# A two-layer mixer block on one core: norm sums on other engines, rows of their own for one branch, and a last-row-last order

## The reference

```python
def _rmsnorm(x, g):
    x32 = x.astype(jnp.float32)
    y = x32 * lax.rsqrt(jnp.mean(jnp.square(x32), axis=-1, keepdims=True) + EPS)
    return (y * g.astype(jnp.float32)).astype(x.dtype)

def _layernorm(x, g, b):
    mu = jnp.mean(x32, axis=-1, keepdims=True)
    var = jnp.mean(jnp.square(x32 - mu), axis=-1, keepdims=True)
    y = (x32 - mu) * lax.rsqrt(var + EPS) * g.astype(jnp.float32) + b.astype(jnp.float32)
...
    ys = (_short_conv(a_b, a_c, a_u, conv_a) @ w_a_out,
          y_b @ w_b_out,
          (jax.nn.gelu(r_g) * rec) @ w_c_out,
          _conformer_conv(d_v, d_g, conv_d, conv_d_b, ln_d_g, ln_d_b) @ w_d_out)
    out = _merge(gl, ys, w_out)
...
        x = x + gt1 * o
        x = x + gt2 * _swiglu(_modulate(x, g_ffn[l], sh2, sc2), w_ffn_in[l], w_ffn_out[l])
...
    return _rmsnorm(x, g_final)
```

## Time and profile before

| What | Value |
| --- | --- |
| median of 3 runs | 2089.33 us (2087.57 to 2090.14) |
| profiled execution | 2084.34 us |
| span in it | 2082.5 us |
| TensorE busy | 2036.4 us, 98% |
| VectorE, ScalarE, GpSimd busy | 1105.7, 877.5, 817.1 us |
| granted TensorE clock | 0.996 of full speed |

### The profile page before, as it was taken

The page is one execution under the profiler, slowest core; times in us unless marked ns, Lnnn a source line. Parts: engine busy times, 40 slices in busy tenths (PEclk is TensorE's granted clock), DMA queues, the critical chain, the costliest instruction groups (busy, mean ns, idle before and its releaser), DMA issues.

```text
span 2082.5 us, 30660 instructions
## 1 busy us (share of the span) xinstructions
PE 2036.4 (98%) x11738; PEld 1700.8 (82%) x11738; DVE 1105.7 (53%) x2031; ACT 877.5 (42%) x1369; POOL 817.1 (39%) x355
## 2 busy tenths in 40 slices
PE   5999999999999999999999999999999999999998
PEld 3778788888877778777777778777999999999998
DVE  5896454567788632123111111479755887644555
ACT  4786344232222333134221222369755434545444
POOL 1003322343434334334343343510446887344443
PEclk9999999999999999999999999999999999999999
DMA  7222211222222222664634422322333455454554
GB/s 312 93 81 82 79 52 55 90 90 101 83 99 81 101 63 100 242 243 182 242 122 170 173 82 101 132 91 82 121 123 121 171 194 184 161 171 160 190 188 142
DMA packets 38705, 278.45 MB, mean 134 GB/s; under 512 B 4416, under 2 KB 4416, under 8 KB 5312
## 3 DMA queue, kind: packets, MB, share of 16 engines
q1 hardware_dynamic: 38592, 276.87, 37.2%
HBM read 275.80 MB, written 1.05 MB: 133 GB/s over the span
## 4 chain that ended last, share of the span: by engine, by line
PE 89%; DVE 5%; ACT 2%; DMA 1%; issue 1%; POOL 1%; SPq 0%; DVEq 0%; ACTq 0%; POOLq 0%
PE PS L473 86%; PE PS L562 2%; DVE PS L1270 1%; ACT WH L838 1%; PE PS L737 1%; POOL WL L433 1%; DVE ZL L1267 1%; DMA RAW<-in_stream 1%; DVE TMP L1273 0%; DMA X<-in_xT 0%; DMA CD<-in_lruw 0%; DVE PS L1267 0%; DVE CD L1270 0%; ACT TMP L838 0%; ACT ZH L838 0%
## 5 line engine op out<-in xcount | busy, mean ns | idle before, releaser
L433 POOL TENSOR_TENSOR WL<-RAW,WH 128x1024 fp32r<-128x1024 f32 x336 | 805.8, 2418 | 1240.8 <-ACT WH L838 1240.8
L473 PE MATMUL PS<-HH,WH 128*128 128x512 f32 (+1 forms) x2272 | 799.5, 352 | 8.2 <-DVE HL L1270 3.4
L473 PE MATMUL PS<-HL,WH 128*128 128x512 f32 (+1 forms) x2272 | 778.2, 343 | 0.0
L473 PE MATMUL PS<-HH,WL 128*128 128x512 f32 (+1 forms) x2272 | 778.0, 342 | 0.0
L838 ACT ACTIVATE WH<-RAW 128x1024 fp32r<-128x1024 f32 x416 | 417.4, 1052 | 723.8 <-PE PS L473 687.8
L473 PEld LDWEIGHTS PS<-HH,WH 128*128 128x128 f32 x2272 | 428.1, 188 | 79.0 <-issue 23.3
L473 PEld LDWEIGHTS PS<-HL,WH 128*128 128x128 f32 x2272 | 428.5, 189 | 57.4 <-issue 5.5
L473 PEld LDWEIGHTS PS<-HH,WL 128*128 128x128 f32 x2272 | 428.0, 188 | 55.6
L473 PE MATMUL PS<-ZH,WH 128*128 128x512 f32 (+1 forms) x992 | 337.7, 340 | 6.3 <-DVE ZL L1267 4.7
L473 PE MATMUL PS<-ZH,WL 128*128 128x512 f32 (+1 forms) x992 | 335.5, 338 | 0.0
L473 PE MATMUL PS<-ZL,WH 128*128 128x512 f32 (+1 forms) x992 | 335.5, 338 | 0.0
(11 more groups left out here) (165 smaller groups left out, 1504.4 us busy)
## 6 DMA issues: line engine op xcount, KB each, us to landing
RAW<-in_stream SPq DMA_DIRECT2D x208, 1024.0 KB, 4.8
CD<-in_modw SPq DMA_DIRECT2D x42, 1024.0 KB, 7.7
CD<-in_lruw SPq DMA_DIRECT2D x2, 2048.0 KB, 8.1
X<-in_xT SPq DMA_DIRECT2D x2, 1024.0 KB, 7.3
S<-in_modw SPq DMA_DIRECT2D x2, 1024.0 KB, 13.0
G<-in_modw SPq DMA_DIRECT2D x2, 1024.0 KB, 21.0
RAW<-in_modw SPq DMA_DIRECT2D x1, 1024.0 KB, 16.0
TMP<-in_modw SPq DMA_DIRECT2D x1, 1024.0 KB, 17.9
```

The lines of the kernel that those rows point to most:

```text
L433: nc.gpsimd.tensor_tensor(WL[:, a:b], RAW[:, a:b], WH[:, a:b].bitcast(F32), ALU.subtract)\
L473: return nc.tensor.matmul(out, lhs, rhs, start=start, stop=stop)
```

## The change

It has seven parts.

1. **Opening norm.** ScalarE squares into five buffers instead of two; TensorE adds the eight rows itself with eight all-ones float32 matmuls of 512 columns, after six more small ones issued early (`keep_warm(6)`); root and reciprocal are of 128x512 and there are no diagonals and no spread. The table for the root is loaded ahead of the squares.
2. **Other norms.** The diagonals are made by ScalarE (`diagonals` in `norm_root`, so ahead of the `high` that follows), no longer by VectorE.
3. **Order.** In the first slabs of w_out and ff_out (both tiles from Z) rows 0 to 6 of both tiles come first, then row 7 of both.
4. **Branch b in layer 2.** It has rows of its own in Z (offset NX), copied row by row during c_out.
5. **a_cu in layer 1.** The output banks are given free by the first product, not by the last low part.
6. **LayerNorm.** VectorE adds the 8 rows (and the 8 squares) with 7 additions each; TensorE keeps one all-ones matmul for each.
7. **a_out in layer 2.** GpSimd forms both halves of WL.

```diff
-POOL_WHOLE = ("c_in", "kv", "q", "d_in", "c_out", "b_out", "a_cu", "a_b", "w_out")
+POOL_WHOLE = ("c_in", "kv", "q", "d_in", "c_out", "b_out", "a_cu", "a_b", "a_out", "w_out")
...
-            pe.wait_ge(L[0]["n1_s"].sem, KC - 1)
-            token_sums(tmp(1), NT, True, True).then_inc(L[0]["n1_p"].sem, 1)
-            spread(L[0]["n1_v"].sem, NT).then_inc(L[0]["n1_p"].sem, 1)
+            keep_warm(6)
+            for k in range(KC):
+                pe.wait_ge(L[0]["n1_a"].sem, k + 1)
+                mm(bank(7), ONES, SQUARES[k % len(SQUARES)], k == 0, k == KC - 1)\
+                    .then_inc(L[0]["n1_p" if k == KC - 1 else "n1_s"].sem, 1)
...
+                if before is not None and ops[0][0] in (Z, Z2):
+                    for rows in (range(nk - 1), range(nk - 1, nk)):
+                        for t, (z, w) in enumerate(ops):
+                            for k in rows:
+                                if t == 0:
+                                    before(k)
...
+                                last = products(s, t, z, w, k, nk)
...
-                for k in range(KC):
-                    last = mm(bank(4, W), ONES, row(CD, k, W), k == 0, k == KC - 1)
-                last.then_inc(lp.sem, 1)
+                pe.wait_ge(lv.sem, lv.at(0, f"a{KC - 1}"))
+                mm(bank(4, W), ONES, tmp(4, 0, W), True, True).then_inc(lp.sem, 1)
                 stage(l, "a_out", [(H, W), (Z, W)], pairs=(1, 2))
-                pe.wait_ge(la.sem, la.at(0, f"q{KC - 1}"))
-                for k in range(KC):
-                    last = mm(seqs(bank(5, W), seqs_of(l)), ONES, padded(k, seqs_of(l)), k == 0, k == KC - 1)
-                last.then_inc(lp.sem, 1)
+                pe.wait_ge(lv.sem, lv.at(0, f"v{KC - 1}"))
+                mm(bank(5, W), ONES, tmp(4, 0, W), True, True).then_inc(lp.sem, 1)
...
+            def diagonals(inverse, m):
+                act.wait_ge(inverse, 1)
+                for c in range(m):
+                    fn(tmp(1, c * P, (c + 1) * P), IDENT, ACT.Identity, scale=tmp(0, m + c, m + c + 1)).then_inc(inverse, 1)
...
+                        gate("co")(n, s, m)
+                        fn(row(ZH, n, W, NX), row(CD, n, W), ACT.Copy).then_inc(a["bz_h"].sem, 1)
...
+                    if l:
+                        dve.wait_ge(a["bz_h"].sem, a["bz_h"].at(n, "z"))
+                        z_low(n, W, row(CD, n, W), NX).then_inc(a["bz_l"].sem, 1)
...
                     tt(seq[:, 0:C, PAD:PAD + NX], seqs(tmp(s, 0, W), C), seqs(bank(2 * s + 1, W), C), MUL)\
-                        .then_inc(*((slab_out[s], 1) if l else (sv.sem, 1)))
+                        .then_inc(slab_out[s], 1)
...
-                        z_low(n, W, tmp(2 + s, 0, W)).then_inc(slab_out[s], 1)
+                        z_low(n, W, tmp(2 + s, 0, W)).then_inc(sv.sem, 1)
...
+                def row_sums(name, at, part):
+                    for k in range(1, KC):
...
+                        tt(seqs(tmp(4, 0, W) if k == KC - 1 else part, C), at(0) if k == 1 else seqs(part, C), at(k), ADD)\
+                            .then_inc(lv.sem, 1)
+                dve.wait_ge(a["cd"].sem, KC * TAPS_D)
+                row_sums("a", lambda k: seqs(row(CD, k, W), C), bank(4, W))
                 stage(l, "a_out", gated("ao"), some=(0, 1))
...
                     tt(row(CD, k, W), row(CD, k, W), bank(4, W), SUB).then_inc(lv.sem, 1)
+                row_sums("v", lambda k: padded(k, C), bank(6, W))
                 stage(l, "a_out", gated("ao"), some=(1, 2))
```

More of the change, by code:

```diff
@@ L514, in slab @@
                     return
+                if before is not None and ops[0][0] in (Z, Z2):
[4 more added lines that the diff above has]
+                                    before(k)
+                                if t == 0 and k == KC // 2 and halves == 1:
+                                    second_half(m, s)
+                                last = products(s, t, z, w, k, nk)
+                            if nk - 1 in rows:
+                                last.then_inc(tile_done[s], 1)
+                            elif t == 0:
+                                for slot, u in mods:
+                                    mod_products(slot, u)
+                    mod_columns_of(mods)
+                    return
                 for j, t in enumerate(order):
@@ L517, in slab @@
                     for k in range(nk):
-                        if before is not None and z is Z and (t == 0 or ops[0][0] is not Z):
+                        if before is not None and z in (Z, Z2):
                             before(k)
@@ L795, in _ @@
                 for s in range(2):
-                    slab(b, s, [(H, W), (Z, W)], order=(1, 0) if s else (0, 1), halves=1)
-                stage(l, "b_out", [(H, W), (Z, W)], before=lambda k: pe.wait_ge(a["bz_l"].sem, a["bz_l"].at(k, "z")))
+                    slab(b, s, [(H, W), (Z, W)], order=(1, 0) if s and l == 0 else (0, 1), halves=1)
+                stage(l, "b_out", [(H, W), (Z2 if l else Z, W)], before=lambda k: pe.wait_ge(a["bz_l"].sem, a["bz_l"].at(k, "z")))
                 stage(l, "a_cu", [(H, W), (H, W)])
@@ L1298, in low, with z_low @@
                 tt(WL[:, x], RAW[:, x], WH[:, x].bitcast(F32), SUB).then_inc(lo_done[1][s], 1)
-            def z_low(n, w, src):
-                return tt(row(ZL, n, w), src, row(ZH, n, w).bitcast(F32), SUB)
-            def inverse(done, chunks):
-                V.reciprocal(tmp(0, chunks, 2 * chunks), tmp(0, 0, chunks)).then_inc(done, 1)
-                dve.wait_ge(done, 1)
-                for c in range(chunks):
-                    ts(tmp(1, c * P, (c + 1) * P), IDENT, tmp(0, chunks + c, chunks + c + 1), None, MUL).then_inc(done, 1)
+            def z_low(n, w, src, at=0):
+                return tt(row(ZL, n, w, at), src, row(ZH, n, w, at).bitcast(F32), SUB)
             def decay_rates(l):
@@ L1379, in _ @@
                         dve.wait_ge(x_loaded[s], 16)
-                    sums, squared = a["n1_s"].sem, a["n1_a"].sem
-                    for k in range(1, KC):
-                        dve.wait_ge(squared, k + 1)
-                        if k > 1:
-                            dve.wait_ge(sums, k - 1)
-                        tt(tmp(1), tmp(1), SQUARES[k % 2], ADD).then_inc(sums, 1)
                     rows = G[:, :].rearrange("p (k n) -> p k n", n=GW)
@@ L1704, in _ @@
                     conv_d(conv_taps("c_out", n))
[L1705 removed]
+                    if n == KC - 1 and l == 0:
                         for k in range(KC):
```

96 lines of the change are left out of this document (55 added, 41 removed).

## The result

The changed kernel takes 2065.54 us (median of 4 runs, 2062.7 to 2067.43) beside 2088.45 us for the kernel before (4 runs, 2087.09 to 2090.14): a ratio of 0.9889, 95% interval 0.9872 to 0.9906, or 22.9 us less by the medians. Forecast were 27.3 us less, 2062 us.

The account below looks back on a forecast made before the run. TensorE, busy 98%, was taken as the bound, so only less work or fewer waits help. Terms -11.3 - 3.3 - 6.5 - 2.6 - 3.5 - 2.2 + 2.15 = -27.3 us from 2089.3 gave 2062 us, range 2056 to 2071.

Parts of the forecast that it names:

- LayerNorm, layer 1: 14 of 16 all-ones records go, twice, with VectorE's additions covered and nothing new late: -11.3 us.
- My price of a record: One all-ones record in layer 1's LayerNorm costs TensorE 6.47/16 = 0.404 us.
- a_cu, branch b, order: Waits for low parts go: layer 1's a_cu -3.5 us, layer 2's b_out -2.6; Z's row 7 asked for later, -2.2.
- Opening: Round 0 starts near 18 us, round 1 at 23.3, bound by DMA: -6.5 us, taken from -5.2 to -7.2.
- Diagonals: Norms between stages: `high` now waits for ScalarE's diagonals; +1.1 us, +0.75 and +0.3, sum +2.15 us.
- LayerNorm, layer 2, and GpSimd's double share: Layer 2's row sums win -3.3 us of 5.7, TensorE standing some 3.4 us at tile 6; double share costs 0.
- Price 0: GpSimd forming both weight halves in layer 2's a_out costs nothing, with 0.9 us of cover.
- My bound of -1.5 us: Layer 2's LayerNorm wins only this if branch d's low parts overlap GpSimd's longer work; they took 7.83 us.
- signs that I had named as wrong: TensorE waiting for TMP at the all-ones matmul, for WL in layer 2's a_out, or a granted clock below 0.99.
- The clock: Rival, slower than before: the standstill at layer 2's tile 6 keeps the clock low; one dip costs 1.7 us; chance 0.02.
- The lock: Rival: each low part in c_out waits for a whole GpSimd half, 2.4 us; total 2072 us; chance 0.03.
- Layer 2 gives back its gains: Rival: faster TensorE runs into the weights' loop, losing 3.3 + 2.6 + 2.0 us; total 2070 us; chance 0.10.

Follow-up runs that it names:

- norm1_by_tensor: The changed kernel with layer 1's norm alone back to TensorE's own sums, mean and variance; 2078.38 us, ratio 0.9948.
- diag_dve: The changed kernel with the diagonals of the norms before ff_in and of layer 2's first norm made by VectorE again; 2062.26 us, ratio 0.9869.
- norm2_by_tensor: The changed kernel with both sums of layer 2's norm back to TensorE, GpSimd's share as changed; 2066.24 us, ratio 0.9888.
- after_again: The changed kernel run and profiled once more on another chip, nothing edited; 2063.96 us, ratio 0.9882.
- after: The first profiled execution of the changed kernel, the slowest of its four; 2067.43 us.
- half_dve: The changed kernel with a_out's low weight parts of layer 2 half on GpSimd and half on VectorE, as before; 2061.47 us, ratio 0.9869.
- warm7: The changed kernel plus seven all-ones products of 256 columns in the standstill of layer 2's LayerNorm; 2065.44 us, ratio 0.9889.

## Why the prediction was right, and where it was wrong

The time is inside the range and the sign and size are right, 22.9 to 25.5 us by the medians of two chips against 27.3. Step by step:

- *LayerNorm, layer 1.* Right, and slightly small: 12.0 us in two steps of 6.0 for 11.3, confirmed by norm1_by_tensor (the table's 12.2 has 0.1 us that norm1_by_tensor shows too). My price of a record was too low. The records start 0.43 us apart (720.50 to 720.93 in the kernel before), but the product behind the last one starts 0.03 us after it and is itself the longer, 0.80 instead of 0.40 us, and it did so in the earlier trace rows too. So 6.47/16 leaves part of the last record out; 14 x 0.43 is 6.0. In layer 2 it is 0.215 us and 3.0 for my 2.85. No wait for TMP stands there; the cover for VectorE's sums was as counted.
- *a_cu, branch b, order.* Right within 0.1, 0.1 and 0.3 us.
- *Opening.* The mechanism is right: round 0 at 19.31 (forecast near 18), round 1 at 24.18 (23.3), round 3 at 36.37 (35.3 to 37.3), with the DMA as the bound. It is -5.8 us where the lower clock fell into rounds 0 or 1, which wait for transfers anyway, and -3.9 where it reached into c_in's first slab. Of the 11 traces of kernels with the warm-up, 6 gained 5.3 to 6.0 us here and 5 gained 3.4 to 4.0. Both ends are within my bounds (0 to -7.5), but -3.9 is outside the -5.2 to -7.2 that I took, which had no price for a lower clock behind the rounds; -6.5 was at the favourable side.
- *Diagonals.* +0.9 us in layer 1 (forecast +1.1), and this is partly luck. By diag_dve the diagonals themselves cost 1.6 us there; the norm without them is 0.65 us shorter than in the kernel before, where the lower clock (951.07 to 954.49 us) made TensorE's spread 1.92 us long, for 1.16 in diag_dve, and VectorE's rows stood behind it. I had not counted that gain. Before ff_in of layer 2 it is +1.5 to +1.9 for +0.75: the lower clock lay there as well in both traces and made the first slab 0.6 us longer, which I had not counted.
- *LayerNorm, layer 2, and GpSimd's double share.* Here the prediction was wrong: -3.3 and 0 forecast, +2.6 and -0.5 measured. The step on the row sums holds by itself: the two steps of 2.9 to 3.0 us came, and TensorE stands 3.31 us at slab 6 (forecast 3.4), so -3.2 us at slab 6; norm2_by_tensor against after_again shows 3.4 us for the sums. The reciprocal's 0.45 us came too: slab 6 stands 0.4 to 0.7 us better with GpSimd's whole share than with half (after and after_again against half_dve). The step that failed is "Price 0" for the double share. I counted cover for the weights only, and they were never late there (no wait for WL in a_out). What I left out is who else is on SBUF. Of the eight low parts of Z for d_out, one met a GpSimd instruction in the kernel before (its half from 1807.75) and all took 4.97 us; four met one when GpSimd worked for all but 1.6 us of them, and they took 9.49 us. TensorE waited 1.87 us, and the clock fell behind it for another 1.5 us. My bound of -1.5 us named this overlap, but sized it by the 7.83 us of the earlier trace rows and had no price for the clock. The pairs of the second table put the double share at 3.7 us, and at 3.2 to 3.9 where both sums are there and the fall behind S is taken off. None of the signs that I had named as wrong came (no wait for TMP or for WL there, a granted clock of 0.994 over the run), so they would not have caught this.
- *The clock.* The prediction put a fall behind the standstill at 1.7 us and within the range. It came in 4 of 6 traces with the full standstill, at 1.4 to 2.4 us each; behind the wait for ZL it came in 7 of 7, at 0.9 to 1.5 us. It never stayed low. That is part of the shortfall, and no rival held it as a cost of more than one place.
- *The lock.* Its mechanism is what happened; its place and price were wrong, and I gave it 0.03. The reading against it was a mean: 0.98 us for a low part in the earlier trace rows is five of 0.41 us, one of 1.13 and two of 2.62 and 2.57, and the long ones end 0.28 us behind the end of a GpSimd instruction of 2.5 to 2.7 us. So it is for every low part of 256 columns out of CD in all 13 traces, and the other way too: a GpSimd instruction that starts just ahead of such an end takes 2.5 to 2.6 us instead of 2.4. The Trainium skill, "SBUF — State Buffer", section "Who interferes with whom", has a VectorE instruction with two SBUF inputs and a GpSimd one that reads SBUF exclude each other for the whole of an instruction; the traces agree. But a low part waits only for what is left of the one instruction that it meets. In c_out each came 0.8 us before GpSimd's first half ended, took 1.10 us and was in time, so part 4 lost nothing of what this rival priced. In d_out's rows, where I priced nothing, three whole GpSimd instructions stood in the way.
- *Layer 2 gives back its gains.* Only in a trifle: one new wait for WL in a_cu, 0.25 us and a restart, and +0.6 us in all over b_out to a_b.

What stays open: why the clock falls behind one standstill of 3.3 us and not behind the next of the same length; why it fell behind the 1.85 us wait for ZL each time, while the kernel before kept its clock behind the 1.87 us wait at b_out and the 1.66 us wait in w_out; and whether warm7's seven products helped, since after_again kept its clock without them. Nor is it known what starts or ends the slow pace of the ff stages.

## What to carry to other kernels

Moving work to an idle engine is free only if the instructions that will now run beside it are looked at too: list the VectorE instructions with two SBUF inputs that fall into GpSimd's new stretch, and count the GpSimd instructions that they will meet, not the VectorE ones. Each one met costs the rest of its length, here up to 2.2 us, and a mean over a merged row hides this; look at the single lengths. Then follow it up to the wait that ends last. A wait of TensorE of 2 to 3 us is to be priced with the lower clock that may follow it, here 1 to 2.4 us more when it came. And a saving on TensorE is worth nothing where another chain ends last anyway: the variance's sums in layer 2 took 2.9 us off TensorE, slab 6 started no earlier, and they opened a standstill behind which the clock fell in 4 of 6 traces.

## What the runs showed that I had not expected

The granted clock falls to the lower level for 3.4 us, sometimes for 6.8, after stretches in which TensorE had stood or was thinly used: behind the 1.85 us wait for ZL in every one of 7 traces, behind 3.3 to 3.7 us of standstill in 4 of 6, and not once in those 33 us in the 4 traces where neither wait was there. The length of a wait alone does not decide it: behind 1.87 us at b_out the kernel before kept its clock. In the opening it matters where it lands: in a round that waits for a transfer it costs nothing, in the first slab behind it 2 us.

At a granted clock of 1.00, products of 256 columns can start 0.120 us apart instead of 0.117 for hundreds in a row; it came in the ff stages of some executions and not of others of the same kernel, and is worth up to 3.2 us of 2065. A single trace of each kernel would have put it down to the change.

A row of a merged timeline can hide two kinds of instruction. Eight low parts in 9.49 us look like eight slow instructions. One by one they are either undisturbed (0.41 us) or held until a GpSimd instruction ends (2.6 us).
